# First two layers: pairs of column tiles with both parts of x in one matmul of 512 columns, and a quarter of the long convolution filtered on GpSimd

## The chip, the cores and the metric

The kernel runs on one core of one Trainium2 chip. The time is device microseconds of one launch, and lower is better. PE is TensorE, DVE VectorE, ACT ScalarE, POOL GpSimd, SP SyncE.

## The reference, cut to what matters

One sequence of 256 positions of width 2048 passes through four layers in fp32. The change touches the first two, which are alike:

```
h = rms_norm(x, norm_w[l])
p = h @ w_in[l]                                   # 2048 x 6668 columns
qa, ka, va, za, ub, zb, qkv_c, b_c, a_c, zc = _split_cols(p)
oa = sliding_window_sink_attention(...) * silu(za)
ob = conformer_conv_module(ub, ...) * silu(zb)    # depthwise convolution, 31 taps, 512 channels
oc = rms_norm(gated_deltanet(qkv_c, b_c, a_c, ...)) * silu(zc)
x = x + concatenate([oa, ob, oc]) @ w_out[l]

def conformer_conv_module(u, conv_w, conv_b, ln_w, ln_b, pw_w, pw_b):
    a, gt = jnp.split(u, 2, axis=-1)
    h = a * jax.nn.sigmoid(gt)
    h = causal_depthwise_conv(h, conv_w) + conv_b.astype(h.dtype)
    h = jax.nn.silu(layer_norm(h, ln_w, ln_b))
    return h @ pw_w + pw_b
```

Layers three and four (a pooling mixer and a gated linear recurrence, with their own large projections) are not touched.

## The kernel before, in words

**Precision by parts.** Every large product is fp32 made from two rounded parts of each factor. A weight chunk W (1 MB: four tiles of 128 rows by 512 columns, or eight by 256) comes by DMA from SP, ACT copies its upper part to WH (`high`, L1125), and DVE subtracts to get its lower part WL (`low`, L1818, over the same memory as W). The activations stand likewise as H: for each 128 rows kt, 256 columns of upper part (HH) and 256 of lower part (HL), side by side. A product is WL by HH plus WH by HL plus WH by HH.

**Two ways to issue it.** In mode "cm" of the class `Group` the weights are stationary and each of the three products is a matmul of 256 columns that adds to one half of a PSUM bank. So one tile of 128 by 128 weights takes three weight loads and three matmuls. Mode "wide" is used by the third and fourth layer: WL meets HH in a matmul of 256 columns, and WH meets both parts in one matmul of 512 columns, so a tile takes two loads and two matmuls, and two partial sums come out, which are added outside TensorE. A wide chunk runs all its WL matmuls and all its WH matmuls in two runs, with the order turned round from chunk to chunk.

**What runs in what order.** `plan()` lists 408 chunks, and every engine walks the list by itself. PE goes through a chunk and calls `pump()` four times in it; each call lets the side work (delta rule `delta_net`, `attention`, `conformer`, `decays`) issue its next small step, at a place counted with `rest(n)`. DVE and ACT have a `tick()` per chunk: first `low` or `high` for the chunk three ahead, then four pumps of their own side work. `group(n)` is n ticks and then a wait for the end of the chunk. All engines issue strictly in their own order, and wait on semaphores.

**PSUM.** The large products use bank pairs in turn by group number g. Group g + 2 may start when what was evicted from group g is done (`released`). In the first two layers a group of 512 columns is four chunks. DVE evicts it with `scaled` (L1783): one op of 128 by 512 for each bank, which multiplies by the row factors RBT of the normalisation. The side work has the other four banks.

**The convolution.** `conformer` on ACT starts the accumulator ACC, four tiles of 128 channels by 256 positions, with the last of the 31 taps, and DVE adds the other 30 taps with one `scalar_tensor_tensor` for each tile (L1787, out QA, in Q, TB, QA), one for each pump, at half that pace for the first 28. The layer's attention comes after it.

```
                for k in range(30):
                    for m in range(4):
                        wk = TB[:, wo + 4 * k + m:wo + 4 * k + m + 1]
                        stt(ACC[:, m, :], HB[:, m, k:k + 256], wk, ACC[:, m, :], ALU.mult, ALU.add, lag=3 if k else m)
                        yield
                        if 4 * k + m < 28:
                            yield
```

In the names of the profile Q and QA are large shared buffers: Q holds the values and masks of the side work, the pool and recurrence buffers, HB and RAW; QA holds ACC and the attention's q and k. SM holds small tiles.

Of the kernel before, what the change touches and what calls it, by code (L numbers as in the profile page):

```python
# [24 lines left out]
        "lo", "ev_v", "norm_v", "dn_v", "cf_v", "at_v", "y_v", "x_v", "uc_v", "d_v", "z_v", "step_v", "post_v")  # L25
# [7 lines left out]
def plan():  # L33
# [6 lines left out]

    for i in range(NP):
        ch.append(("w_in", 0, piece(i)[0], PIECES[i], 2048, 512))
    for l in range(2):
        for c in (2048, 2560)[1 - l:]:
            cols("w_in", l, c, 512)
        cols("w_vba", l, 0, 268)
        for c in (3584, 4096, 4608, 5120):
            cols("w_in", l, c, 512)
        cols("w_in", l, 5632, 256, step=8)
        cols("w_in", l, 5900, 512)  # L50
        cols("w_in", l, 6412, 256, step=8)
        for c in (3072, 0, 512):
            cols("w_in", l, c, 512)
        cols("w_in", l, 1280, 512)
# [193 lines left out]
def program(nc, wall, tab, pos_d, pT_d, xin, xT_d, gpost_d, gplo_d, xsave, out):  # L248
# [6 lines left out]
    with ctx:  # L255
# [10 lines left out]
        UL1 = ctx.enter_context(nc.sbuf_tensor("UL1", [128, 2, 256], F32R))  # L266
        QA = ctx.enter_context(nc.sbuf_tensor("QA", [128, 3584], F32))
# [45 lines left out]
        POOL_G, LRU_G = range(41, 84), range(93, 128)  # L313
        LAST_G = range(LRU_G.stop, LRU_G.stop + 8)

        def bank(g, b):
# [6 lines left out]
            return PS[:, 1024 * (g % 2) + 512 * b:1024 * (g % 2) + 512 * b + 512]  # L323

# [11 lines left out]
        DIAG = pair(SM[:, 704:960])  # L336
        ROPE = SM[:, 64:96]
# [112 lines left out]
        def tensor(e, w):  # L450
# [152 lines left out]

            def turn(n, i, *ready):
# [15 lines left out]
            def first_opening():  # L620
# [5 lines left out]
                def total():  # L626
                    yield from rest(1)
# [7 lines left out]
                g = Group(from_h, lambda kt: [hl_of(0, kt)], 512, "cm", 16)  # L635
                begin(total())
                g.feed(hi_first=True)
                g.all()
# [307 lines left out]
            def block1(l):  # L946
                if l:
                    opening(1, (3, "ev_v", 19))
# [17 lines left out]
                proj(l, 512)  # L966
# [4 lines left out]
                proj(l, 512)  # L971
                finish(cf)
                Group(lambda kt: ACC[:, kt, :], lambda kt: [("cf_a", l, "silu")], 512, "cm", 4).all()
                proj(l, 256)
# [10 lines left out]
                n, g16 = l + 1, 20 * l + 16  # L985
# [25 lines left out]
            def pool_layer():  # L1011
                assert here["g"] + 1 == POOL_G[0]

                def load_u(g):
                    if g:
                        proj(2, 512, "wide")
                    else:
                        opening(2, (3, "ev_v", 39))
# [82 lines left out]
        def scalar(e, w):  # L1101
# [61 lines left out]

            def skip(n):
# [22 lines left out]
            def entry(n):  # L1187
# [5 lines left out]
                g16 = 20 * n - 4  # L1193
# [155 lines left out]
            def attention(l):  # L1349
# [44 lines left out]
                w.wait_ge(*to("ev_v", 20 * l + 15))  # L1394
# [10 lines left out]
            def block1(l):  # L1405
                if l:
                    tick()
                    upper(1, 3)
                    sumsq(1, 3, SQX, X, ("ev_v", 19))
# [25 lines left out]
                cf = begin(conformer(l, skip(4)))  # L1435
# [11 lines left out]
                for i in range(5):  # L1447
                    g = skip(4 if i < 4 else 2)
# [4 lines left out]
                for k, (n, t0, t1) in enumerate(((4, 10, 14), (2, 14, 16))):  # L1453
                    begin(gate(Y[:, t0:t1, :], skip(n), "dn_a", l, "zc", k))
                begin(gate(Y[:, 6:10, :], skip(4), "cf_a", l, "zb"))
# [8 lines left out]
                skip(4)  # L1464
# [5 lines left out]
                group(2)  # L1470
# [5 lines left out]
                for k in (6, 8):  # L1476
                    ysplit(k, k // 2 - 3, "ev_v", 20 * l + 14)
# [45 lines left out]
            def pool_layer():  # L1523
# [240 lines left out]
        def vector(e, w):  # L1764
# [175 lines left out]

            def summed(dst, g):
# [174 lines left out]
            def conformer(l):  # L2116
# [15 lines left out]
                half = CFT[:, 0:512]  # L2132
                tt(half.rearrange("p (m c) -> p m c", m=2), ACC[:, 0:2, :], ACC[:, 2:4, :], ALU.add)
# [110 lines left out]
            def block1(l):  # L2244
# [5 lines left out]
                g = group(4)  # L2250
# [395 lines left out]
```

## Time and profile before

| what | value |
|---|---|
| median of 3 runs | 2366.91 us (2366.69 to 2366.96) |
| the profiled execution | 2367.18 us, of which the span is 2365.4 us |
| PE | 2346.3 us busy, 99% of the span |
| PE weight loads | 2091.4 us, 88% |
| DVE | 1675.6 us, 71% |
| ACT | 1283.1 us, 54% |
| POOL | 0.2 us |

The granted TensorE clock is 1.00 in every stretch read below. A busy share is the union of an engine's instructions; two engines that are busy at once are both counted.

### The profile page before, as it was taken

The numbers are of one execution on the slowest core, as the hardware profiler recorded it, in microseconds if no ns is written. First come the engines' busy times: TensorE is split into PE (matmuls) and PEld (weight loads), VectorE is DVE, ScalarE is ACT, GpSimd is POOL, SyncE is SP. The second block draws the span as 40 slices with busy tenths as digits, with TensorE's granted clock in tenths as the row PEclk, the third lists the DMA queues.
The fourth block names the chain that finished last, engine by engine and source line by source line (L and its number), as shares of the span: only waits on it lengthen the run. The fifth ranks groups of instructions, "written<-read, shape, count | busy, mean of one in ns | idle before, by whom it ended". The sixth has DMA issues, their size and how long they took to land.

```text
span 2365.4 us, 35787 instructions
## 1 busy us (share of the span) xinstructions
PE 2346.3 (99%) x15332; PEld 2091.4 (88%) x15332; DVE 1675.6 (71%) x1922; ACT 1283.1 (54%) x1434; POOL 0.2 (0%) x4
## 2 busy tenths in 40 slices
PE   9999999999999999999999999999999999999997
PEld 9999898899998988988888888888888888888886
DVE  7888768558986685667567576676668668678774
ACT  6554366545543655444434334475566575667573
POOL 0000000000000000000000000000000000000000
PEclk9999999999999999999999999999999999999999
DMA  7543334555533345555555555565455555555553
GB/s 266 204 179 132 120 143 156 191 217 186 179 125 124 136 170 196 187 192 193 187 190 196 189 185 195 193 221 194 145 196 183 191 196 186 188 196 187 202 204 119
DMA packets 64558, 428.03 MB, mean 181 GB/s; under 512 B 7184, under 2 KB 7824, under 8 KB 15504
## 3 DMA queue, kind: packets, MB, share of 16 engines
q1 hardware_dynamic: 61568, 414.48, 48.7%
q10 hardware_dynamic: 2832, 11.27, 1.3%
q8 instruction: 120, 1.97, 0.3%
q14 instruction: 38, 0.31, 0.0%
HBM read 421.53 MB, written 4.19 MB: 180 GB/s over the span
## 4 chain that ended last, share of the span: by engine, by line
PE 97%; DVE 2%; ACT 1%; issue 0%; DMA 0%; DVEq 0%; ACTq 0%
PE PS L456 95%; PE PS L616 1%; ACT Q L1111 1%; DVE Q L1783 0%; PE PS L914 0%; PE PS L748 0%; DVE X L1787 0%; PE PS L735 0%; DVE Q L1787 0%; PE PS L895 0%; DVE SM L1802 0%; DVE H L1783 0%; DVE E L1783 0%; DMA W<-in_wall 0%; ACT L1111 0%
## 5 line engine op out<-in xcount | busy, mean ns | idle before, releaser
L1818 DVE TENSOR_TENSOR WL<-W,WH 128x2048 fp32r<-128x2048 f32 (+3 forms) x406 | 887.7, 2194 | 453.9 <-ACT WH L1125 453.2
L1125 ACT ACTIVATE WH<-W 128x2048 fp32r<-128x2048 f32 (+3 forms) x406 | 740.9, 1836 | 492.1 <-PE PS L456 430.7
L456 PE MATMUL PS<-H,WH 128*128 128x256 f32 (+1 forms) x4864 | 868.9, 325 | 0.7 <-ACT H L1111 0.7
L456 PEld LDWEIGHTS PS<-H,WH 128*128 128x128 f32 x4864 | 740.7, 191 | 72.5 <-ACT WH L1125 0.8
L456 PE MATMUL PS<-H,WL 128*128 128x256 f32 x3392 | 491.3, 284 | 0.1
L456 PEld LDWEIGHTS PS<-H,WL 128*128 128x128 f32 x3392 | 446.5, 192 | 8.0 <-issue 1.8
L456 PE MATMUL PS<-WH,H 128*128 128x512 f32 (+1 forms) x1280 | 331.2, 379 | 0.0
L456 PEld LDWEIGHTS PS<-WH,H 128*128 128x128 f32 x1280 | 234.1, 188 | 46.0
L456 PE MATMUL PS<-WH,YS 128*128 128x512 f32 x1024 | 273.8, 389 | 0.0
L456 PEld LDWEIGHTS PS<-WH,YS 128*128 128x128 f32 x1024 | 192.2, 188 | 40.0
L456 PE MATMUL PS<-WL,H 128*128 128x512 f32 (+1 forms) x640 | 197.6, 388 | 0.1
L1111 ACT ACTIVATE Q<-PS 128x512 f32<-128x512 f32 (+3 forms) x134 | 68.9, 552 | 187.5 <-PE PS L456 119.4
L456 PE MATMUL PS<-WL,YS 128*128 128x512 f32 x512 | 157.8, 389 | 0.0
L456 PEld LDWEIGHTS PS<-WL,H 128*128 128x128 f32 x640 | 114.7, 188 | 22.6 <-issue 2.0
L456 PEld LDWEIGHTS PS<-WL,YS 128*128 128x128 f32 x512 | 95.5, 188 | 19.5 <-issue 0.2
L1787 DVE SCALAR_TENSOR_TENSOR QA<-Q,TB,QA 128x256 f32<-128x256 f32 x240 | 107.5, 477 | 0.1
L1783 DVE TENSOR_TENSOR Q<-Q,PS 128x512 f32<-128x512 f32 (+1 forms) x90 | 54.8, 648 | 63.3 <-ACT Q L1111 34.1
L1787 DVE SCALAR_TENSOR_TENSOR Q<-Q,TB 128x256 f32<-128x256 f32 x206 | 93.9, 491 | 7.7 <-ACT Q L1111 6.9
L456 PEld LDWEIGHTS PS<-Q 64*64 64x64 f32 (+2 forms) x1440 | 65.8, 149 | 9.7 <-issue 7.8
L1111 ACT ACTIVATE Q<-Q 128x1024 f32<-128x1024 f32 (+4 forms) x50 | 56.9, 1137 | 29.2 <-DVE Q L1792 11.8
L456 PE MATMUL PS<-Q 64*64 64x64 f32 (+2 forms) x1440 | 72.2, 240 | 0.0
L1111 ACT ACT_TABLE_LOAD x48 | 61.6, 1283 | 1.6
(164 smaller groups left out, 1634.9 us busy)
## 6 DMA issues: line engine op xcount, KB each, us to landing
W<-in_wall SPq DMA_DIRECT2D x374, 1024.0 KB, 4.8
W<-in_wall SPq DMA_DIRECT2D x22, 512.0 KB, 3.5
W<-in_wall SPq DMA_DIRECT2D x8, 536.0 KB, 3.4
X<-in_x ACTq DMA_DIRECT2D x1, 2048.0 KB, 9.5
xsave<-X ACTq DMA_DIRECT2D x1, 2048.0 KB, 8.5
X<-xsave ACTq DMA_DIRECT2D x1, 2048.0 KB, 9.7
Q<-in_g_post ACTq DMA_DIRECT2D x8, 256.0 KB, 3.5
Q<-in_g_ple_out ACTq DMA_DIRECT2D x2, 1024.0 KB, 4.5
```

The costliest lines, as they stand in the source:

```text
L456: return e.matmul(o, l, r, start=start, stop=stop, skip_group_check=True)
L616: o = e.transpose(b[:, 256 * j + 128 * t:256 * j + 128 * t + 128], X[:, t, c:c + 128], ident)
L1111: e.activation(o, a, f, **k).then_inc(*up(*sig))
L1125: e.activation(WH[:, s % NSPL, 0:m], W[:, c % NRAW, 0:m], ACT.Copy).then_inc(*up("hi", c))
L1783: e.tensor_tensor(o, a, b, op).then_inc(*after(sig))
L1787: e.scalar_tensor_tensor(out=o, in0=a, scalar=s, in1=b, op0=op0, op1=op1).then_inc(*after(sig))
L1818: e.tensor_tensor(WL[:, c % NRAW, 0:m], W[:, c % NRAW, 0:m], WH[:, s % NSPL, 0:m].bitcast(F32), ALU.subtract).then_inc(*up("lo", c))
```

## The change

In the first two layers every part of the input product (h by w_in) that was in mode "cm", but for the first 512 columns of each layer, becomes mode "wide" in groups of 256 columns: 19 such pairs of column tiles in each layer, 38 in all, of two chunks each. A chunk is then eight row tiles by 256 columns instead of four by 512; its bytes and the number of chunks stay. Groups for v, the decays, q, k and the output product stay as they were.

A pair is evicted by two engines. ACT copies the second half of both banks (the sum of WL by HH and WH by HL) to a new tile PART; DVE adds PART to the first half into the destination, and then multiplies the destination by RBT, two ops of 128 by 512 where there was one. PART has one buffer, so ACT's copy waits until DVE has used the last one. PE waits for the eviction of a group of 256 columns, two chunks long, where it was one of four chunks.

The fourth tile of the convolution is filtered by GpSimd: for each of 30 taps a `tensor_scalar` into a small tile TAP, and a `tensor_tensor` that adds it to the accumulator, each waiting for the one before. DVE keeps three tiles and its pace of pumps, and waits for GpSimd's last tap before it sums the tiles. One side step (`total`) is placed one pump later.

```diff
+    def pairs(l, c0):
+        for c in (c0, c0 + 256):
+            cols("w_in", l, c, 256, step=8)
...
+        PART = nc.alloc_sbuf_tensor_at("PART", [128, 2, 256], F32, offset=nc.sbuf_base - 4 * 512)
...
+        def both(g, k):
+            v = PS[:, 1024 * (g % 2):1024 * (g % 2) + 1024]
+            return v.rearrange("p (i k t) -> p i k t", i=2, k=2)[:, :, k, :]
...
+        TAP = SM[:, 704:960]
...
             # tensor
+            def pairs(n, ncols):
+                for _ in range(ncols // 256):
+                    proj(n, 256, "wide")
...
-                for _ in range(3):
-                    proj(l, 512)
+                pairs(l, 3 * 512)
                 finish(dc)
                 dn = begin(delta_net(l), first=True)
-                proj(l, 512)
-                proj(l, 256)
-                proj(l, 512)
-                proj(l, 256)
-                proj(l, 512)
+                pairs(l, 512 + 256 + 512 + 256 + 512)
                 proj(l, 512, "tm")
                 proj(l, 512, "tm")
...
             # scalar
+            def pairs(n):
+                for _ in range(n):
+                    g = group(2)
+                    if "pair" in here:
+                        w.wait_ge(*to("ev_v", here["pair"]))
+                    here["pair"] = g
+                    act(PART[:, :, :], both(g, 1), ACT.Copy, "ev_a", g)
+                return g
...
             # vector
+            def pairs(dst, n):
+                for b in range(n):
+                    g = group(2)
+                    w.wait_ge(*to("ev_a", g))
+                    tt(dst(b), both(g, 0), PART[:, :, :], ALU.add)
+                    tt(dst(b), dst(b), rb(2), ALU.mult, "ev_v", g)
...
                 for k in range(30):
                     for m in range(4):
-                        wk = TB[:, wo + 4 * k + m:wo + 4 * k + m + 1]
-                        stt(ACC[:, m, :], HB[:, m, k:k + 256], wk, ACC[:, m, :], ALU.mult, ALU.add, lag=3 if k else m)
+                        if m < 3:
+                            wk = TB[:, wo + 4 * k + m:wo + 4 * k + m + 1]
+                            stt(ACC[:, m, :], HB[:, m, k:k + 256], wk, ACC[:, m, :], ALU.mult, ALU.add,
+                                lag=2 if k else m)
                         yield
                         if 4 * k + m < 28:
                             yield
                 half = CFT[:, 0:512]
+                w.wait_ge(*to("tap_g", l, 29))
...
+        def gpsimd(e, w):
+            for l in range(2):
+                w.wait_ge(*to("near"))
+                w.wait_ge(*to("cf_v", l, "hb"))
+                w.wait_ge(*to("cf_a", l, "acc"))
+                for k in range(30):
+                    wk = AT["b_conv_w"] + 124 * l + 4 * k + 3
+                    if k:
+                        w.wait_ge(*to("tap_g", l, k - 1))
+                    e.tensor_scalar(TAP, HB[:, 3, k:k + 256], TB[:, wk:wk + 1], None, ALU.mult).then_inc(
+                        *up("mul_g", l, k))
+                    w.wait_ge(*to("mul_g", l, k))
+                    e.tensor_tensor(ACC[:, 3, :], ACC[:, 3, :], TAP, ALU.add).then_inc(*up("tap_g", l, k))
```

What moves is seen best in the engines' own orders. On PE, just ahead of the first layer's v and decay product, the "cm" rows of before read as follows (H is x, L456 the matmul helper, x the count of equal instructions):

```order
L456 MATMUL PS<-H,WL 128x256 x4
L456 MATMUL PS<-H,WH 128x256 x8
L456 MATMUL PS<-H,WL 128x256 x4
L456 MATMUL PS<-H,WH 128x256 x8
L646 MATMUL PS<-TB,RBT 128x128 x2
L456 MATMUL PS<-WL,H 128x268 x2
```

The same place now:

```order
L470 MATMUL PS<-H,WH 128x512 x24
L470 MATMUL PS<-H,WL 128x256 x32
L470 MATMUL PS<-H,WH 128x512 x32
L470 MATMUL PS<-H,WL 128x256 x16
L662 MATMUL PS<-TB,RBT 128x128 x2
L470 MATMUL PS<-WL,H 128x268 x2
```

Twelve matmuls for four tiles have become four of 256 and four of 512 columns, in long runs of one kind.

On DVE, in the delta rule of the first layer, the transposed keys (Q<-PS,SM) were followed at once by `low` and the solver's first step (Q<-PS,TB). Before:

```order
L1783 TENSOR_TENSOR Q<-PS,SM 128x512 x3
L1787 SCALAR_TENSOR_TENSOR QA<-Q,TB,QA 128x256 x2
L1783 TENSOR_TENSOR Q<-PS,SM 128x2x128 x6
L1787 SCALAR_TENSOR_TENSOR QA<-Q,TB,QA 128x256 x2
L1818 TENSOR_TENSOR WL<-W,WH 128x2048
L1783 TENSOR_TENSOR Q<-PS,TB 128x384 x2
```

Now:

```order
L1804 TENSOR_TENSOR Q<-PS,SM 128x512 x3
L1808 SCALAR_TENSOR_TENSOR QA<-Q,TB,QA 128x256 x2
L1804 TENSOR_TENSOR Q<-PS,SM 128x2x128 x6
L1808 SCALAR_TENSOR_TENSOR QA<-Q,TB,QA 128x256
L1804 TENSOR_TENSOR Y<-PS,PART 128x512
L1804 TENSOR_TENSOR Y<-Y,RBT 128x512
L1839 TENSOR_TENSOR WL<-W,WH 128x2048
L1804 TENSOR_TENSOR Q<-PS,TB 128x384 x2
```

One tap op is gone there, and a pair's eviction of two ops stands ahead of the solver's step. Twenty rows earlier another eviction has grown from one op to two.

On DVE in the first layer's attention, the third place, before (Y<-PS,RBT is the last eviction of the layer's input product, H<-Y,H the split of the mixer's output, Q<-PS,TB the next heads' scores):

```order
L1783 TENSOR_TENSOR Y<-PS,RBT 128x512
L1783 TENSOR_TENSOR H<-Y,H 128x2x256 x3
L1818 TENSOR_TENSOR WL<-W,WH 128x2048
L1787 SCALAR_TENSOR_TENSOR Q<-PS,TB 128x384 x4
```

Now:

```order
L1804 TENSOR_TENSOR Y<-PS,PART 128x512
L1804 TENSOR_TENSOR Y<-Y,RBT 128x512
L1804 TENSOR_TENSOR H<-Y,H 128x2x256 x3
L1839 TENSOR_TENSOR WL<-W,WH 128x2048
L1808 SCALAR_TENSOR_TENSOR Q<-PS,TB 128x384 x4
```

One op more stands ahead of the scores.

## Rows read from the trace of the kernel before

**Rows 1.** The page: span, busy time by engine, the chain that ended last

```profile
span 2365.4 us, 35787 instructions
PE 2346.3 (99%) x15332; PEld 2091.4 (88%) x15332; DVE 1675.6 (71%) x1922; ACT 1283.1 (54%) x1434; POOL 0.2 (0%) x4
PE 97%; DVE 2%; ACT 1%; issue 0%; DMA 0%; DVEq 0%; ACTq 0%
```

**Rows 2.** Waits of PE in the whole span: total us, times, longest

```profile
PE PS L616 <- DVE X L1787: 4.0, 1, 4.0
PE PS L456 <- DVE RBT L1810: 1.2, 1, 1.2
```

**Rows 3.** Timeline of PE in a "cm" group: start us, us, instructions, count

```profile
500.47 1.12 PE L456 MATMUL PS<-H,WH 128*128 128x256 f32 x8
...
501.91 0.76 PE L456 MATMUL PS<-H,WH 128*128 128x256 f32 x5
```

**Rows 4.** Timeline of PE in "wide" groups of the third layer

```profile
1106.79 4.00 PE L456 MATMUL PS<-H,WL 128*128 128x256 f32 x32
1110.62 7.44 PE L456 MATMUL PS<-H,WH 128*128 128x512 f32 x32
1117.91 2.31 PE L456 MATMUL PS<-H,WL 128*128 128x256 f32 x18
```

**Rows 5.** Groups by form: count, busy us, mean ns, idle before

```profile
L1787 DVE SCALAR_TENSOR_TENSOR QA<-Q,TB,QA 128x256 f32<-128x256 f32 x240 | 107.5, 477 | 0.1
...
L1111 ACT ACTIVATE Q<-PS 128x512 f32<-128x512 f32 x84 | 46.1, 597 | 116.4 <-PE PS L456 89.1 <-PE PS L914 18.1 <-PE PS L895 9.1
...
L1783 DVE TENSOR_TENSOR Y<-PS,RBT 128x512 f32<-128x512 f32 x20 | 13.1, 687 | 7.6 <-PE PS L456 6.6
...
L1792 DVE TENSOR_SCALAR Q<-Q,TB 128x256 f32<-128x256 f32 x32 | 9.1, 347 | 0.0
...
L1783 DVE TENSOR_TENSOR Q<-PS,SM 128x256 f32<-128x256 f32 x12 | 4.2, 416 | 0.2
```

**Rows 6.** Windows of layer one: length, PE, PEld, DVE, ACT, POOL, clock, DMA

```profile
60.00:120.00 60.00, 60.00 (x503) 60.00 (x502) 50.94 (x90) 32.10 (x39) 0.00 (x0) 1.00 0.53 195
120.00:160.00 40.00, 40.00 (x335) 40.00 (x335) 33.50 (x51) 16.82 (x13) 0.00 (x0) 1.00 0.50 185
160.00:200.00 40.00, 40.00 (x305) 37.13 (x304) 33.00 (x53) 28.06 (x25) 0.00 (x0) 1.00 0.44 158
200.00:245.00 45.00, 45.00 (x470) 44.47 (x471) 43.38 (x62) 14.46 (x11) 0.00 (x0) 1.00 0.35 124
```

**Rows 7.** Timeline: first op on the convolution's accumulator, and the sum of its tiles

```profile
60.07 2.08 ACT L1111 ACTIVATE QA<-Q,TB 128x256 f32<-128x256 f32 x4 [0.22 <-DVE Q L1783]
...
312.10 0.69 DVE L1783 TENSOR_TENSOR Q<-QA 128x512 f32<-128x512 f32 x1
```

**Rows 8.** Timeline, ACT and DVE splitting one weight chunk

```profile
108.55 1.92 ACT L1125 ACTIVATE WH<-W 128x2048 fp32r<-128x2048 f32 x1 [3.84 <-PE PS L456]
...
110.50 2.29 DVE L1818 TENSOR_TENSOR WL<-W,WH 128x2048 fp32r<-128x2048 f32 x1 [1.09 <-ACT WH L1125]
```

**Rows 9.** Timeline at the decays: last softplus op, first matmul on it

```profile
80.48 0.17 DVE L1783 TENSOR_TENSOR SM<-SM 128x12 f32<-128x12 f32 x1
...
83.58 0.51 PE L456 MATMUL PS<-SM,TB 128*128 128x12 f32 x4
```

**Rows 10.** Timeline at the solver's first step

```profile
242.27 1.01 DVE L1783 TENSOR_TENSOR Q<-PS,TB 128x384 f32<-128x384 f32 x2
...
244.24 0.97 PE L456 MATMUL PS<-Q 64*64 64x64 f32 x26
```

**Rows 11.** Timeline at attention's first transposes

```profile
350.92 0.76 DVE L1798 COPY Q<-QA 128x512 f32<-128x512 f32 x2
...
352.83 0.60 PE L895 MATMUL PS<-TB,QA 128*128 128x128 f32 x4
```

**Rows 12.** Timeline at attention's transposed weights, with the wait before

```profile
378.67 0.67 PEld L914 LDWEIGHTS PS<-TB,Q 128*128 128x128 f32 x6 [0.17 <-DVE Q L1787]
```

More of the change, by code:

```diff
@@ L43, in plan @@
     for l in range(2):
-        for c in (2048, 2560)[1 - l:]:
-            cols("w_in", l, c, 512)
+        if l:
+            cols("w_in", l, 2048, 512)
+        pairs(l, 2560)
         cols("w_vba", l, 0, 268)
         for c in (3584, 4096, 4608, 5120):
-            cols("w_in", l, c, 512)
[L49 to L54, printed above, removed]
+            pairs(l, c)
+        cols("w_in", l, 5632, 256, step=8)
+        pairs(l, 5900)
+        cols("w_in", l, 6412, 256, step=8)
+        pairs(l, 3072)
+        for c in (0, 512):
+            cols("w_in", l, c, 512)
+        pairs(l, 1280)
         cols("b_pw_w", l, 0, 512, nkt=4)
@@ L626, in total @@
                 def total():
-                    yield from rest(1)
+                    yield from rest(2)
                     b = side(("norm", 0, "rb"), ("norm_a", 0, "rb"))
@@ L951, in block1 @@
                 if l:
-                    proj(l, 512)
+                    pairs(l, 512)
                 else:
@@ L1434, in block1 @@
                 skip(1)
-                cf = begin(conformer(l, skip(4)))
+                cf = begin(conformer(l, pairs(2)))
                 if not l:
@@ L1463, in block1 @@
                 att = begin(attention(l))
-                skip(4)
+                pairs(2)
                 finish(cf)
@@ L1469, in block1 @@
                 skip(1)
-                group(2)
+                pairs(1)
                 def ysplit(k, lag, *ready):
@@ L2249, in block1 @@
                     rp = begin(rope_tables())
-                g = group(4)
+                pairs(lambda b: Y[:, 6 + 2 * b:8 + 2 * b, :], 2)
                 if not l:
                     finish(rp)
-                scaled(lambda b: Y[:, 6 + 2 * b:8 + 2 * b, :], g)
                 if not l:
@@ L2266, in block1 @@
                 for i in range(5):
-                    g = group(4 if i < 4 else 2)
-                    scaled(lambda b: RAW[:, 4 * i + 2 * b:4 * i + 2 * b + 2, 3:259], g, 2 if i < 4 else 1)
+                    pairs(lambda b: RAW[:, 4 * i + 2 * b:4 * i + 2 * b + 2, 3:259], 2 if i < 4 else 1)
                     begin(taps(l, i, 4 if i < 4 else 2))
@@ L2273, in block1 @@
                 for n, t0 in ((4, 10), (2, 14)):
-                    scaled(lambda b: Y[:, t0 + 2 * b:t0 + 2 * b + 2, :], group(n), n // 2)
-                scaled(lambda b: Y[:, 6 + 2 * b:8 + 2 * b, :], group(4))
+                    pairs(lambda b: Y[:, t0 + 2 * b:t0 + 2 * b + 2, :], n // 2)
+                pairs(lambda b: Y[:, 6 + 2 * b:8 + 2 * b, :], 2)
                 group(4)
@@ L2279, in block1 @@
                 att = begin(attention(l))
-                scaled(lambda b: Y[:, 2 * b:2 * b + 2, :], group(4))
+                pairs(lambda b: Y[:, 2 * b:2 * b + 2, :], 2)
                 finish(cf)
@@ L2291, in block1 @@
                         lag=m)
-                scaled(lambda b: Y[:, 4:6, :], group(2), 1)
+                pairs(lambda b: Y[:, 4:6, :], 1)
                 def add_x(i, g):
```

41 lines of the change are left out of this document (21 added, 20 removed).

## The prediction, made blind

> **What bounds the kernel now.** The page comes first. PE is busy for 2346.3 us of a span of 2365.4, and the chain that ended last lies on it for 97% [rows 1]. The reader should still ask whether this busy engine is a waiting one, since an engine's busy time can hide stalls that others cause. The list of PE's waits answers: beside the start and the end, the two longest kinds are 4.0 and 1.2 us, one wait each [rows 2]. So TensorE works without a break, and every other engine is late only where nobody sees it. What shortens PE's own stream shortens the kernel, as long as the others still keep out of its way. That second half is the hard one here. DVE is busy for 43.38 of the 45 us from 200 to 245 [rows 6], so there it has no room, and the places where PE takes over a DVE result have little to spare [rows 9 to 12]. These are read by eye from the timeline: when the DVE op ends, and when PE's matmul that needs it starts.
>
> **Part 1, fewer matmuls.** In a "cm" group twelve matmuls, four tiles' worth, come every 1.44 us, from 500.47 to 501.91 [rows 3]. That is 360 ns a tile. In a "wide" group 32 matmuls of 256 columns begin at 1106.79, 32 of 512 at 1110.62, and the next run at 1117.91 [rows 4]: 11.12 us for 32 tiles, 347.5 ns a tile. The reader can take the pieces apart: 120 ns for 256 columns, 228 for 512. The streamed columns are the same 768, so only the share that each matmul carries beyond its columns is saved, 12.5 ns a tile. The change moves 38 pairs of column tiles by 16 row tiles, which is 1216 tiles: 1216 x 12.5 ns = 15.2 us. A chunk of 16 tiles then takes 5.56 us instead of 5.76.
>
> The Trainium skill (TensorE: Matmul & The Clock Gate, Back-to-back issue gap) gives an isolated warm matmul N / 2.4 + about 2.5 ns, so a matmul saved would be worth 2.5 ns, and the 1216 would give 3.0 us instead of 15.2. The rows, with a weight load for every matmul, show 13 to 14 ns over the columns' own time at both sizes, so by them the larger figure stands.
>
> **Part 2, the evictions.** A bank cost DVE one op: 13.1 us for 20, 0.655 each [rows 5]. A pair costs two that depend on each other, of 687 ns each and a little for the handover, 1.4 us. Nineteen pairs for each layer add 19 x (1.4 - 0.655) = 14.2 us to DVE. ACT gains 19 copies of 597 ns [rows 5], 11.3 us, and has the room: 32.10 busy of 60 us, 16.82 of 40, 28.06 of 40, 14.46 of 45 [rows 6]. The release of PSUM is not in danger by size: a group lasts 11.1 us now, and copy and two ops need 2.0. It would be late only with DVE 9 us behind.
>
> **Part 3, the taps.** DVE loses 30 taps for each layer. 240 taps take 107.5 us, 0.448 each [rows 5], so 13.4 us. Evictions and taps nearly cancel over a layer, +0.8 us. They don't cancel everywhere: from 60 to 160 us DVE does only 28 of the 120 taps, so it loses 7 (3.1 us) while eight pairs come (6.0 us), and PE is 16 x 0.2 = 3.2 us faster through it. DVE's spare time there, 9.1 + 6.5 = 15.6 us [rows 6], becomes 9.5; from 160 to 200 it has 7.0, less 1.2 for the faster PE. That leaves 15 us for what GpSimd does to it.
>
> **Part 4, GpSimd.** It begins when ACT has started the accumulator, at about 62 us, and has until the tiles are summed at 312 [rows 7], 250 us for 30 taps or 8.3 us each; even at three times DVE's price it is done in time. The trace has no tensor op on POOL (0.2 us, four instructions [rows 1]), so what it does to DVE is bounded: below, nothing; above, every one of the 60 ops holds DVE back for as long as DVE would take for such an op, 347 ns and 416 ns [rows 5], 0.76 us a tap and 23 us a layer. I take 0.4 us a tap, 12 us a layer, the middle of the two bounds, since no row lies nearer to the one than to the other. It fits in the 15 us, barely.
>
> The weight parts forgive this. ACT starts on a chunk at 108.55 and DVE has finished at 112.79 [rows 8]; three chunks of 5.76 lie between, so PE needs it at 125.8, 13.0 us later. With chunks of 5.56, ACT's copy and the longer eviction, 10.4 remain.
>
> **Part 5, the places that don't forgive**, for each layer:
> - Decays: DVE ends at 80.65, PE starts at 83.58, 2.9 us to spare [rows 9]. PE comes 0.6 earlier (three chunks). The softplus ahead is some fifteen short DVE ops in a chain, just when GpSimd is at work; if 9 or 10 of them are held up for 0.38 us, half of the two ops of a tap together, they end 3.5 us later. PE waits 1.2.
> - Solver: DVE ends at 243.28, PE starts at 244.24, 0.96 to spare [rows 10]. Since 200 DVE had no room. It gains 0.1, 0.75 and 1.4 us of evictions and loses about six taps, 2.7 us; PE is 7 x 0.2 = 1.4 us earlier. About 0.3 with ACT's handover.
> - Attention's transposes: 351.68 to 352.83, 1.15 to spare [rows 11]. PE is 0.8 earlier, and ACT's copy of 0.6 stands in the chain that leads there. 0.25.
> - Attention's weights: PE waits 0.17 us already [rows 12]. One op more (0.75) and PE two chunks (0.4) earlier, less what the wait itself rounds off: 1.0.
>
> Sum: 2.75 us a layer, 5.5 for both. 15.2 - 5.5 = 9.7. The profiled execution took 2367.18 us, its span and 1.8 around it, so 2357.5; it stands 0.27 over the median of the runs, so **2357.2 us**.
>
> **The rivals.**
> *Full gain.* DVE takes none of it back, or the waits fall where PE would have waited anyway. 2366.9 - 15.2 = 2351.7. For it: half of the places have ACT or DVE idle just ahead. Against: the wait that is there already [rows 12].
> *GpSimd eats it.* Each tap delays DVE 0.65 us, 20 a layer, 5 more than it has. The delay stands at 200, where DVE can't work it off, and the solver's steps wait for it: about 4.5 us a layer beyond mine, 2366.
> *GpSimd turns it round.* The same mechanism, past its point. From 15 us on, each us of delay in a layer is a us of PE; the gain is gone at 15 + 9.7 / 2 = 20 us a layer, 0.66 us a tap, and the kernel is measurably slower from about 22. If a GpSimd op takes half as long again as DVE's, and always collides, a tap costs 1.14 us, a layer 34, which is 19 over: 2357.2 + 38 = 2395. With the upper bound above it is 2373. For it: the window 60 to 120 is 85% busy with ops that read two SBUF tensors. Against: GpSimd slows itself down in the same way, so that its ops spread out.
> The Trainium skill (SBUF — State Buffer, Who interferes with whom) says that DVE instructions with two SBUF inputs contend with GpSimd instructions that read SBUF, and that the loser blocks for the whole instruction. No row of this trace shows it. The Trainium skill (GPSIMD Engine Reference, 3.1 Elementwise — side-by-side cycle accounting) has the GpSimd's `tensor_tensor` at 1.96 times DVE's time; by both together this rival would be the likeliest, which is why it has the chance it has.
> *The matmuls save little.* 3 us less the waits, 2369. The spacing of the matmuls speaks against it [rows 3, 4], and nothing here for it.
>
> **How the numbers follow.** My forecast 0.62, its own range 2352 to 2362; full gain 0.10; GpSimd eats it 0.14; turns it round 0.11; little saved 0.03. A measurement of this kernel can tell 0.2%, 4.7 us, from no change, so 2362.2 to 2371.6 is the same. Faster: 0.62 + 0.10 = 0.72. Same: 0.14 + 0.03 = 0.17. Slower: 0.11. The range runs from 2351 (the full gain) to 2370, which leaves out the case turned round and the edge of the one before it.
>
> **What would show it.** Right: PE rows of 512 columns 228 ns apart in layers one and two, PE's busy time 8 to 15 us less, new waits of PE on DVE of about a us at the four places. Wrong: waits of PE on WL at 100 to 200 us, or waits in the solver of several us, with DVE's mean for its taps well above 477 ns while POOL is busy. If the pitch of the 512 column matmuls in these layers were 240 ns, part 1 would be wrong.

## The result, and the profile after

The changed kernel takes 2382.92 us (median of four runs, 2382.53 to 2384.25), and the kernel before 2366.89. The ratio is 1.0069, with a 95% interval of 1.0058 to 1.0081. It is 16 us slower where 9.7 us faster was forecast.

The page's totals answer to [rows 1]:

```profile
span 2380.7 us, 33530 instructions
PE 2340.5 (98%) x14116; PEld 2029.4 (85%) x14116; DVE 1706.3 (72%) x1900; ACT 1299.8 (55%) x1472; POOL 153.3 (6%) x124
PE 79%; DVE 13%; ACT 4%; issue 3%; DMA 1%; DVEq 0%; ACTq 0%
```

PE was idle for 19.1 us of the span before and is for 40.2 now, 21.1 more. Its busy time fell by only 5.8. The difference of the two is what the span grew by, 15.3. The chain that ended last lay on PE for 97% and now does for 79%; DVE's part rose from 2% to 13%. The waits of PE, in us in total, times and longest, answer to [rows 2]:

```profile
PE PS L470 <- DVE Q L1804: 9.3, 12, 2.0
PE PS L470 <- ACT Q L1122: 6.7, 2, 3.3
...
PE PS L930 <- DVE Q L1808: 2.3, 4, 0.8
PE PS L751 <- DVE Q L1804: 2.0, 2, 1.0
...
PE PS L470 <- DVE SM L1804: 1.1, 1, 1.1
```

The matmuls did what they should. In the first layer a wide chunk runs as in [rows 4], 7.28 us from the first of 32 matmuls of 512 columns to the next run:

```profile
93.56 7.44 PE L470 MATMUL PS<-H,WH 128*128 128x512 f32 x32
100.84 3.34 PE L470 MATMUL PS<-H,WL 128*128 128x256 f32 x26
```

GpSimd's ops by form:

```profile
L2619 POOL TENSOR_SCALAR SM<-Q,TB 128x256 f32<-128x256 f32 x60 | 92.2, 1537 | 459.8 <-ACT QA L1122 454.1
L2622 POOL TENSOR_TENSOR QA<-QA,SM 128x256 f32<-128x256 f32 x60 | 60.9, 1015 | 5.0
```

It was at work in the first layer from 63.2 to 145.1 us. Here is the window of 62 to 144 us (the columns are those of [rows 6]), and then the same window of the kernel before:

```profile
62.00:144.00 82.00, 78.45 (x460) 69.59 (x459) 72.10 (x99) 41.77 (x47) 75.54 (x59) 0.98 0.51 185
```

```profile
62.00:144.00 82.00, 82.00 (x687) 82.00 (x686) 68.02 (x117) 42.13 (x46) 0.00 (x0) 1.00 0.51 186
```

GpSimd did its 30 taps of the layer back to back, in 82 us. What this cost DVE is read from its groups by form in that window (count, busy us, mean ns), which answer to the means of [rows 5]:

```profile
L1839 DVE TENSOR_TENSOR WL<-W,WH 128x2048 fp32r<-128x2048 f32 x14 | 35.3, 2523 | 6.7 <-ACT WH L1136 6.7
L1808 DVE SCALAR_TENSOR_TENSOR QA<-Q,TB,QA 128x256 f32<-128x256 f32 x20 | 12.2, 627 | 0.0
L1808 DVE SCALAR_TENSOR_TENSOR Q<-Q,TB 128x256 f32<-128x256 f32 x17 | 11.1, 685 | 0.0
L1804 DVE TENSOR_TENSOR Q<-Q,RBT 128x512 f32<-128x512 f32 x5 | 3.9, 789 | 0.2
L1804 DVE TENSOR_TENSOR Q<-PS,PART 128x512 f32<-128x512 f32 x5 | 3.5, 692 | 1.5 <-ACT PART L1122 1.0
...
L1808 DVE SCALAR_TENSOR_TENSOR SM<-SM 128x12 f32<-128x12 f32 x9 | 2.8, 310 | 0.3
```

In the kernel before, the same window has 2288, 477, 477 and 171 ns for the first, second, third and last of these forms. 14 x 0.235, 20 x 0.150, 17 x 0.208, 5 x 0.1 and 9 x 0.139 us make 11.6. Summed over every op of DVE, each against the median of its form without GpSimd, it is 13.4 us in the layer, 0.45 a tap. The expectations below say 13.7. The op that reads a PSUM bank and one SBUF tile, `Q<-PS,PART`, takes 692 ns with GpSimd busy or not.

Where the time went is seen best in PE's progress. PE raises a semaphore at the end of each chunk; its times in the trace, as us behind (+) or ahead (-) of the kernel before at the same chunk, are these. The first layer ends in chunk 79. Each row is of the profiled execution. That of "pairs only" took 2369.50 us, 2.6 under the median of its runs, so its row shows less loss than the median has.

```
chunk                 17     29     33     37     45     66    104    112    120    150
before, ends at     65.1  137.3  160.3  188.5  252.1  410.4  604.4  655.6  719.3  917.4
the changed kernel   0.0   +2.9   +3.1   +6.8   +7.8   +8.0   +7.4  +14.4  +15.3  +15.5
pairs only          -0.3   -2.7   -3.5   -1.6   +2.0   +2.3   -0.9   -1.0   +2.6   +2.9
GpSimd only          0.3    0.7    0.7    0.7    0.7    0.7    1.1    1.1    1.1    1.1
no fourth tile      +0.7   -1.7   -2.5   -3.3   -2.5   -2.2   -5.4   -7.0   -6.2   -5.9
fourth tile late    +0.3   -2.1   -3.0   -3.7   -2.6   -2.4   -5.6   -7.2   -6.1   -5.8
ACT order            0.1   +3.0   +2.2   +2.3   +3.3   +3.5   +4.4   +3.7   +4.7   +5.0
gap in the solver   +0.5   -1.9   -2.7   -3.5   -4.2   -4.5   -7.7   -9.3  -10.0  -10.3
```

Where nothing is in the way, each four chunks bring 0.8 us, 0.2 a chunk, as the prediction had it. The changed kernel loses its time in steps, at the chunks 21, 28, 37 and 42 to 45, and again in the second layer.

### The profile page after: what moved, and what is told of

The parts are those of the page before. It is cut to its first block, busy times and chain, and to the rows that moved or that the text cites. A ratio compares the mean times of both kernels' runs of the same rounds, so it can differ in the third digit from the quotient of the medians.

```text
span 2380.7 us, 33530 instructions
## 1 busy us (share of the span) xinstructions
PE 2340.5 (98%) x14116; PEld 2029.4 (85%) x14116; DVE 1706.3 (72%) x1900; ACT 1299.8 (55%) x1472; POOL 153.3 (6%) x124
## 4 chain that ended last, share of the span: by engine, by line
PE 79%; DVE 13%; ACT 4%; issue 3%; DMA 1%; DVEq 0%; ACTq 0%
PE PS L470 77%; DVE WL L1839 3%; DVE Q L1804 3%; DVE Q L1808 2%; ACT Q L1122 2%; DVE QA L1808 2%; ACT WH L1136 1%; PE PS L634 1%; DMA W<-in_wall 1%; DVE Y L1804 1%; DVE SM L1823 0%; ACT QA L1122 0%; DVE QA L1804 0%; DVE Q L1815 0%; DVE SM L1808 0%
## 5 line engine op out<-in xcount | busy, mean ns | idle before, releaser
L470 PE MATMUL PS<-H,WH 128*128 128x512 f32 (+1 forms) x3648 | 807.0, 376 | 0.3 <-ACT H L1122 0.3
L470 PEld LDWEIGHTS PS<-H,WH 128*128 128x128 f32 x3648 | 649.6, 189 | 118.1 <-issue 0.7
L470 PE MATMUL PS<-H,WL 128*128 128x256 f32 x3392 | 444.6, 284 | 8.1 <-DVE Q L1804 7.5
L470 PEld LDWEIGHTS PS<-H,WL 128*128 128x128 f32 x3392 | 428.5, 192 | 20.0 <-issue 10.3
L470 PE MATMUL PS<-WH,H 128*128 128x512 f32 (+1 forms) x1280 | 331.2, 379 | 0.0
L470 PE MATMUL PS<-WH,YS 128*128 128x512 f32 x1024 | 273.8, 389 | 0.0
L470 PEld LDWEIGHTS PS<-WH,H 128*128 128x128 f32 x1280 | 234.1, 188 | 45.9
L470 PEld LDWEIGHTS PS<-WH,YS 128*128 128x128 f32 x1024 | 192.2, 188 | 40.0
L470 PE MATMUL PS<-WL,H 128*128 128x512 f32 (+1 forms) x640 | 197.7, 388 | 0.0
L1122 ACT ACTIVATE Q<-PS 128x512 f32<-128x512 f32 (+3 forms) x134 | 68.9, 552 | 182.1 <-PE PS L470 118.2
L470 PE MATMUL PS<-WL,YS 128*128 128x512 f32 x512 | 157.8, 389 | 0.0
L470 PEld LDWEIGHTS PS<-WL,H 128*128 128x128 f32 x640 | 114.7, 188 | 22.7 <-issue 2.0
L2619 POOL TENSOR_SCALAR SM<-Q,TB 128x256 f32<-128x256 f32 x60 | 92.2, 1537 | 459.8 <-ACT QA L1122 454.1
L470 PEld LDWEIGHTS PS<-WL,YS 128*128 128x128 f32 x512 | 95.5, 188 | 19.5 <-issue 0.2
L1808 DVE SCALAR_TENSOR_TENSOR Q<-Q,TB 128x256 f32<-128x256 f32 x206 | 100.3, 531 | 7.7 <-ACT Q L1122 6.9
L1804 DVE TENSOR_TENSOR Q<-Q,PS 128x512 f32<-128x512 f32 (+1 forms) x90 | 54.9, 649 | 61.6 <-ACT Q L1122 34.1
L1808 DVE SCALAR_TENSOR_TENSOR QA<-Q,TB,QA 128x256 f32<-128x256 f32 x180 | 88.3, 512 | 0.1
L470 PEld LDWEIGHTS PS<-Q 64*64 64x64 f32 (+2 forms) x1440 | 65.9, 149 | 12.8 <-issue 10.5
L470 PE MATMUL PS<-Q 64*64 64x64 f32 (+2 forms) x1440 | 72.4, 240 | 1.7 <-DVE Q L1804 1.7
L1122 ACT ACTIVATE Q<-Q 128x1024 f32<-128x1024 f32 (+4 forms) x50 | 56.9, 1137 | 30.2 <-DVE Q L1813 11.8
```

The lines of the kernel that those rows point to most:

```text
L470: return e.matmul(o, l, r, start=start, stop=stop, skip_group_check=True)
L1122: e.activation(o, a, f, **k).then_inc(*up(*sig))
L1804: e.tensor_tensor(o, a, b, op).then_inc(*after(sig))
L1808: e.scalar_tensor_tensor(out=o, in0=a, scalar=s, in1=b, op0=op0, op1=op1).then_inc(*after(sig))
L2619: e.tensor_scalar(TAP, HB[:, 3, k:k + 256], TB[:, wk:wk + 1], None, ALU.mult).then_inc(*up("mul_g", l, k))
```

## The experiments

Theory A was that GpSimd's burst alone did it, theory B that the eviction by two engines did. Theories C and D came from the first four runs. Each time stands beside that of the kernel before on the same chip.

**Pairs only.** GpSimd's function is left out and DVE filters all four tiles:

```diff
-                        if m < 3:
-                            ... lag=2 if k else m)
+                        stt(ACC[:, m, :], HB[:, m, k:k + 256], wk, ACC[:, m, :], ALU.mult, ALU.add, lag=3 if k else m)
-                w.wait_ge(*to("tap_g", l, 29))
```

> The changed kernel without its GpSimd part: DVE filters all four tiles again, the 38 pairs stay. Theory A (the burst): GpSimd does its 30 taps of a layer back to back in 82 us, its collisions cost DVE 13.7 us there, DVE falls behind and everything that waits for it is late. Without GpSimd the pairs then bring nearly what their matmuls save, 15.5 us, less waits of some us where DVE is full (200 to 245 us): 2354 to 2358 us. Theory B (the eviction by two engines): two DVE ops and a copy through one PART buffer, with PE waiting two chunks later, is itself what stalls PE, and GpSimd adds little: 2372 or more, with PE's waits on released banks at 127 to 175 us still there.

Measured: 2372.12 us beside 2366.95, ratio 1.0019 (1.0010 to 1.0028). Neither theory's number. The waits on released banks are gone, so B as stated falls; but the pairs alone lose 5 us, and A had them win about 10.

**GpSimd only.** The groups of before, with GpSimd's function, the loop of three tiles and the wait for its last tap from the change.

> The kernel before, with only the fourth convolution tile moved to GpSimd; groups stay as they were. Theory A: the same 60 GpSimd ops a layer collide just as much, DVE is lengthened by 12 to 14 us between 60 and 145 us of the layer, less the 3 us of its taps that went; the 13 us of spare time there just take it, so PE waits little: 2366 to 2370 us. Theory B: GpSimd's share of the loss is small anyhow: 2365 to 2367 us. The split of DVE's lengthening (is it 13.7 us without the pairs too?) is the reading that matters here.

Measured: 2366.86 beside 2366.95, ratio 1.0000 (0.9991 to 1.0008). That lies in both theories' ranges, so the time alone does not tell them apart. The collisions are all there:

```profile
L1820 DVE TENSOR_TENSOR WL<-W,WH 128x2048 fp32r<-128x2048 f32 x15 | 37.0, 2469 | 7.0 <-ACT WH L1127 7.0
L1789 DVE SCALAR_TENSOR_TENSOR Q<-Q,TB 128x256 f32<-128x256 f32 x22 | 14.6, 696 | 0.0
L1789 DVE SCALAR_TENSOR_TENSOR QA<-Q,TB,QA 128x256 f32<-128x256 f32 x21 | 13.8, 673 | 0.0
```

They are 14.9 us in the layer, op by op, and PE does not feel them. So 5 and 0 become 16 only together. That each half takes the room that the other needs is the likely reading; the later runs bear it out.

**No fourth tile.** As the changed kernel, GpSimd's function and the wait for it left out. The fourth tile keeps its first tap only, so a part of the convolution isn't computed.

> The changed kernel with GpSimd's part left out and the fourth tile of the convolution left with its first tap only (its output is therefore not the reference's). DVE has the relief and no collision. Theory A: about 2352 us, the full saving of the matmuls. Theory B: 2370 or more, since the eviction is as in the changed kernel.

Measured: 2360.00 beside 2366.95, ratio 0.9970 (0.9958 to 0.9981). A's sign, not its size: with DVE relieved and nobody colliding, 8 of 15 us are still missing. Its waits of PE say where:

```profile
PE PS L930 <- DVE Q L1808: 2.3, 4, 0.8
PE PS L751 <- DVE Q L1804: 2.0, 2, 1.0
PE PS L470 <- DVE Q L1804: 1.6, 2, 0.8
```

They stand in the solver and ahead of the attention's weights.

**Paced.** GpSimd waits before tap k:

```diff
                 for k in range(30):
+                    w.wait_ge(*to("chunk", (17, 92)[l] + k))
```

> The changed kernel with GpSimd paced: tap k waits for the end of the chunk 17 + k (92 + k in the second layer), so the 30 taps are spread over some 200 us in place of 82. Theory A: the total of DVE's lengthening stays 10 to 14 us a layer, but the spare time of 60 to 200 us takes most of it: 2358 to 2366 us. Theory B: no change, 2380 to 2384 us. If only the sum of collisions counted and not their density, it would also stay near 2383.

Measured: 2380.15, ratio 1.0054 (1.0041 to 1.0068). A falls: the taps are spread over 200 us, and almost nothing comes back. It is the number of B, but B alone had fallen with the first run. Its largest wait of PE has moved to the start of the delta rule:

```profile
186.76 3.78 PE L470 MATMUL PS<-Q,TB 128*128 128x512 f32 x4 [4.04 <-ACT Q L1122]
```

Two theories come from these four. C: what counts is when DVE is loaded. D: DVE and ACT hold each other up in a ring. The next rows are why. In the changed kernel, first ACT, then DVE, from 150 us, when GpSimd has long finished:

```profile
151.98 1.71 ACT L1122 ACTIVATE Q<-Q,TB 128x256 f32<-128x256 f32 x4 [9.05 <-DVE Q L1804]
153.78 1.06 ACT L1122 ACTIVATE Q<-Q 128x1024 f32<-128x1024 f32 x1
154.75 1.90 ACT L1136 ACTIVATE WH<-W 128x2048 fp32r<-128x2048 f32 x1
```

```profile
150.53 0.69 DVE L1804 TENSOR_TENSOR Q<-PS,PART 128x512 f32<-128x512 f32 x1
151.25 0.69 DVE L1804 TENSOR_TENSOR Q<-Q,RBT 128x512 f32<-128x512 f32 x1
151.86 2.29 DVE L1839 TENSOR_TENSOR WL<-W,WH 128x2048 fp32r<-128x2048 f32 x1
154.06 1.27 DVE L1808 SCALAR_TENSOR_TENSOR QA<-Q,TB,QA 128x256 f32<-128x256 f32 x3
156.68 2.29 DVE L1839 TENSOR_TENSOR WL<-W,WH 128x2048 fp32r<-128x2048 f32 x1 [1.35 <-ACT WH L1136]
```

The reader follows it in a circle. ACT stands for 9.05 us in `taps`, waiting for DVE's late eviction. Behind it in ACT's order is `high`, the copy to WH. ACT has been idle since 142.9. The copy could have started at 146.40, when PE ended chunk 30, and yet it starts only at 154.75; now DVE, which is late, has to wait 1.35 us for it. So DVE idles while it is behind, and does not catch up. In the kernel before the same ACT op waits 0.4 to 1.2 us.

**ACT order.** The changed kernel, with that op of ACT one chunk later for four of five groups, behind the next `high`:

```diff
             def taps(l, i, n, g):
-                yield
+                yield from rest(5 if i < 4 else 1)
...
-                yield from rest(3 * n + 6)
+                yield from rest(3 * n + 2 if i < 4 else 3 * n + 6)
```

> The changed kernel with one edit in ACT's order: the first operation of the delta rule's short filters, which waits for DVE's eviction, stands one chunk later, behind the next weight part's copy. In the changed kernel ACT stood idle for 9 us at it with that copy queued behind, and DVE then waited 1.35 us for the copy. Theory D (DVE and ACT hold each other up in a ring): DVE catches up after GpSimd's taps, and the time falls by 3 to 8 us, to 2375 to 2380. Theory C alone (DVE's load): 2382 to 2384, unchanged, and if ACT becomes late with the filters, more.

Measured: 2371.89 beside 2366.79, ratio 1.0021 (1.0012 to 1.0029), 11 us less than the changed kernel. D is shown, and is worth more than expected. GpSimd still works in a burst (to 147.7 us) and collides as much (14.1 us), but the window of 120 to 160 us has DVE busy for 39.23 us, where the changed kernel had 35.73; first the changed kernel, then this run:

```profile
120.00:160.00 40.00, 37.40 (x201) 32.49 (x200) 35.73 (x42) 20.28 (x21) 23.50 (x19) 0.96 0.47 163
```

```profile
120.00:160.00 40.00, 37.98 (x207) 33.26 (x206) 39.23 (x48) 19.97 (x20) 26.08 (x19) 0.96 0.48 174
```

Of DVE's 4.3 idle us 3.7 were waits for `high`; in this run none are. PE's waits of 3.3 us for ACT at the delta rule's start are 0.6 to 0.7 us now, and all its waits in the row `PE PS L470 <- DVE Q L1804` fall from 9.3 to 5.9 us.

**Same pace.** The changed kernel, GpSimd's tap k held back to about DVE's tap k:

```diff
+                    w.wait_ge(*to("chunk", (17, 92)[l] + (2 * k if k < 5 else k + 5)))
```

> The changed kernel with GpSimd's tap k held back until about where DVE does its own tap k (a tap for every two chunks at first, then one a chunk, last one after chunk 51 of the layer). Theory C: the lengthening of DVE stays at 13 to 15 us a layer and now stands where the relief of 13.4 us stands, so both cancel and the time is that of the run with pairs and no GpSimd, 2369 to 2375 us. If a collision costs more than it lasts, because it meets ops that others wait for (the solver's), 2378 us or more.

Measured: 2380.06, ratio 1.0051 (1.0037 to 1.0065), the higher of the two numbers, and a miss for C. DVE was lengthened by less than expected here, 9.5 us in the first layer and 11.0 in the second, so it is not the sum of collisions that keeps the time up. **Pace and ACT order** is the same with the edit to `taps`:

> GpSimd at DVE's pace, with the same edit in ACT's order. Theory C and D together: with the ring open, collisions and relief cancel, and the time is that of the run with pairs, no GpSimd and the same order, within 3 us. Its own stall at 182 us (4.0 us for ACT) goes: 2361 to 2368. If collisions cost more than they last, because of what they hit: 2372 or more.

Measured: 2366.41 beside 2367.20, ratio 0.9998 (0.9989 to 1.0007), in the expected range. **Pairs and ACT order** has DVE filter all tiles, with the edit:

> Pairs with all four tiles on DVE at their old places and no GpSimd, plus the edit in ACT's order of the run before (the short filters' first operation one chunk later). Theory D: the loss of the pairs alone was the ring too (ACT idled 7 us at 159 to 166, PE then waited 2.4 us for it at 183 and the clock fell at 216), so it turns from 5 us over the kernel before into a gain: 2361 to 2366 us. If DVE's plain load was the cause, 2370 to 2373, unchanged.

Measured: 2367.79 beside 2367.20, ratio 1.0002 (0.9993 to 1.0011), above the 2361 to 2366 expected, but 4 us below the pairs alone. Here are the differences of these medians to the kernel before, in us; each is uncertain by 2 to 3 us:

```
                          ACT's order as it was    with the edit
pairs, all on DVE                 +5.2                  +0.6
GpSimd at DVE's pace             +13.3                  -0.8
GpSimd at once (the change)      +16.0                  +5.1
```

Read down the second column: with the ring open, that is with the edit that breaks it, GpSimd's collisions cost about what the taps relieve (-0.8 beside +0.6), and the burst costs some 6 us more. That this is because it comes before the relief is argued from its place. Read across: the ring is worth 5, 14 and 11 us, more where GpSimd makes DVE late. What is left of the pairs' loss stands at DVE in the solver. Of the pairs with ACT's order, these are PE's two waits there in the first layer, and then the window:

```profile
213.07 2.02 PE L470 MATMUL PS<-Q 128*128 128x128 f32 x16 [1.99 <-DVE Q L1804]
235.46 1.77 PE L751 MATMUL PS<-TB,Q 128*128 128x128 f32 x8 [2.19 <-DVE Q L1804]
```

```profile
200.00:245.00 45.00, 40.83 (x323) 36.27 (x323) 44.01 (x64) 13.65 (x13) 0.00 (x0) 0.96 0.28 98
```

**Fourth tile late.** Pairs, no GpSimd, ACT's order as it was. DVE does the fourth tile's taps behind the others', from the 22nd on:

```diff
+                        j = 4 * (k - 21) + m
+                        if 0 <= j < 30:
+                            stt(ACC[:, 3, :], HB[:, 3, j:j + 256], wk, ACC[:, 3, :], ALU.mult, ALU.add,
+                                lag=1 if m < 3 else 0)
```

> Pairs as in the changed kernel, GpSimd unused; DVE filters three tiles at their old places, and the 30 taps of the fourth tile stand behind them in DVE's order from the 22nd tap on (about 252 to 312 us of the layer). Theory C (what counts is when DVE is loaded: until 245 us it has no room, in 245 to 320 it idles 27 of 75 us): the 13.4 us of taps are hidden there, and the time is that of the run that left the tile out, 2358 to 2362 us. If DVE's total load counted, or the solver's steps had no room for 0.4 us ahead of them, it would be the 2372 us of the run with all four tiles on DVE.

Measured: 2361.72 beside 2366.79, ratio 0.9977 (0.9968 to 0.9987). C holds. The 13.4 us of taps a layer cost 1.7 us in all over the run that left them out (2360.00), by the medians, which is within the uncertainty of the two. The window of 245 to 320 us takes them; before, then this run:

```profile
245.00:320.00 75.00, 75.00 (x879) 63.70 (x876) 47.52 (x70) 30.90 (x36) 0.00 (x0) 1.00 0.33 124
```

```profile
245.00:320.00 75.00, 75.00 (x839) 62.17 (x838) 55.42 (x87) 32.79 (x40) 0.00 (x0) 1.00 0.32 113
```

**Last 256 columns as before.** The same, and columns 1792 to 2047 in mode "cm" with one DVE op (`proj(l, 256)` on PE, `group(2)` on ACT, `scaled(..., group(2), 1)` on DVE).

> As the run with the fourth tile late on DVE, and the last group of 256 columns of each layer's input product (columns 1792 to 2047) is again issued with separate 256-column matmuls and evicted by one DVE op. It gives up 0.4 us of TensorE a layer and takes one op of 0.7 us and a wait for ACT out of DVE's order ahead of the attention's scores. Theory C: PE's waits on DVE there (1.1 us a layer) fall to 0.3, so the time is 0.5 to 1.5 us below that run. If these waits have another cause it is 0.8 us above.

Measured: 2360.28, ratio 0.9971 (0.9959 to 0.9982). 1.4 us less, as expected, though no more than the two runs' spread. The wait for the attention's weights is the shown part: 2.2 us in four waits became 0.7 in two.

**Solver's groups as before.** In addition the three groups of columns 5900 to 6667:

> As the run with the fourth tile late and the last 256 columns of the product by separate matmuls, and three more groups of 256 columns for each layer (5900 to 6667, those that DVE evicts ahead of and in the solver) issued so too. It gives up 3 x 0.4 = 1.2 us of TensorE a layer and takes three DVE ops of 0.7 us from the stretch of 189 to 245 us, where DVE is full and PE waits 0.8 and 1.0 us. Theory C: the waits go, 2.3 us a layer with what restarting costs, so 1 us a layer is left: 2357 to 2360. If the waits move to the next step of the solver, 2361 to 2363.

Measured: 2359.43 beside 2367.20, ratio 0.9967 (0.9955 to 0.9980). The wait of 0.8 us went, that of 1.0 became 0.5, and the 2.4 us given up on PE ate what that brought. No difference to the run before that can be told.

**Gap in the solver.** Fourth tile late and the last 256 columns as before; no taps on DVE from the 15th to the 21st, and all that are left in the 36 steps from the 22nd on:

```diff
+                        if k < 14:
+                            if m < 3:
+                                tap(m, k, 2 if k else m)
+                        elif i >= 0:
+                            for t in later[13 * i // 6:13 * (i + 1) // 6]:
+                                tap(*t, 1)
```

> As the run with the fourth tile late and the last 256 columns by separate matmuls, but DVE does no taps at all from the 15th to the 21st (about 190 to 250 us of the layer, the solver's first half), and does the 27 + 21 + 30 taps that are left in the 36 steps from the 22nd on (about 252 to 312 us). Theory C: DVE has 9 us more room where PE waits for it (0.8, 1.0 and 0.2 us), so these waits go, and 31 us of taps with 39 of other work fit in the 76 us that follow: 2355 to 2358 us. If the steps of the solver that stand between the taps come late there, new waits at 250 to 310 us of the layer: 2361 us or more.

Measured: 2356.97 beside 2366.81, ratio 0.9958 (0.9944 to 0.9971). This is the fastest version, 9.8 us ahead of the kernel before. DVE's room has moved to where PE waits for it, and of the solver's three waits in a layer one is left:

```profile
200.00:245.00 45.00, 44.49 (x390) 39.17 (x388) 38.94 (x53) 13.11 (x12) 0.00 (x0) 1.00 0.34 119
245.00:320.00 75.00, 75.00 (x838) 62.07 (x838) 61.01 (x104) 34.33 (x41) 0.00 (x0) 1.00 0.32 113
```

```profile
231.25 1.25 PE L751 MATMUL PS<-TB,Q 128*128 128x128 f32 x8 [0.51 <-DVE Q L1804]
```

## Why the prediction was wrong

**Part 1 was right.** 228 ns for 512 columns, 0.2 us a chunk. The figure of the Trainium skill (TensorE: Matmul & The Clock Gate, Back-to-back issue gap) for an isolated matmul, about 2.5 ns beyond its columns, would have given 0.04 us a chunk. It does not fit this stream.

**Part 4's price was right, and its sum wrong.** 0.4 us a tap, 12 a layer, was forecast; 13.4 was measured. There is luck in that. The upper bound charged each GpSimd op with DVE's time for it, 0.35 and 0.42 us, and the shortest that GpSimd took were 0.92 and 0.72, so the bound was none, and its middle no more than a good guess. The step that failed is "it fits in the 15 us, barely". It failed twice. First, these 15 us were counted up to 200 us, but GpSimd, which after the accumulator's start waits for nobody, had finished by 145. Up to 144 DVE had had 14 us of idle time (82 less 68.02), of which the prediction's own working had already given some 6 to the pairs and the faster PE. Second, that idle time was not spare. The busy share says how long an engine did nothing, not that it could have worked: DVE was waiting for ACT's `high` then, and once DVE was late ACT waited for DVE in turn. The run with ACT's order shows the part of the ring: 11 of the 16 us.

Forecast and result lie 25.7 us apart. One way from the result back to the forecast goes through the runs: opening the ring takes off 11 us (+16.0 to +5.1), holding GpSimd to DVE's pace 6 (to -0.8), and doing the taps on DVE, but out of the solver's stretch, with the last 256 columns as before, 9 (to -9.8). Another order of the steps would share it out otherwise.

A count in part 3 was off as well. From 60 to 160 us the kernel before has 43 of the 120 tap operations, not 28. That made DVE's room look some 1.7 us smaller than it was, so it doesn't explain the loss.

**Part 2 had the danger and dismissed it.** "It would be late only with DVE 9 us behind." It was. The eviction of chunks 24 and 25, which ended at 114.10, began on DVE at 125.55, 11.4 us later, and PE, which needed the banks for chunk 28, waited for it:

```profile
125.55 0.69 DVE L1804 TENSOR_TENSOR Q<-PS,PART 128x512 f32<-128x512 f32 x1
```

```profile
127.27 2.80 PE L470 MATMUL PS<-H,WL 128*128 128x256 f32 x16 [2.02 <-DVE Q L1804]
```

The next one, of chunks 26 and 27, began 13.6 us after their end (125.27, 138.86), and PE waited again, for 0.15 to 0.4 us each, at every second chunk until 175. The prediction's signs of being wrong had waits for WL in this stretch and not for banks; of these signs only the mean of the taps (627 ns) came true.

**Part 5's list was short by its worst place.** It named hand-overs from DVE to PE only. At the delta rule's start PE waits for ACT to read its sums (L1122, `Q<-PS,TB`), and ACT came there late because its order runs through DVE's eviction. ACT first, then PE:

```profile
186.57 0.91 ACT L1122 ACTIVATE Q<-Q,TB 128x256 f32<-128x256 f32 x2 [1.72 <-DVE Q L1804]
187.39 1.89 ACT L1136 ACTIVATE WH<-W 128x2048 fp32r<-128x2048 f32 x1
189.30 1.28 ACT L1126 ACT_TABLE_LOAD   x1
190.59 3.01 ACT L1122 ACTIVATE Q<-PS,TB 128x512 f32<-128x512 f32 x5
```

```profile
191.34 1.99 PE L470 MATMUL PS<-Q,TB 128*128 128x512 f32 x4 [3.34 <-ACT Q L1122]
```

Of the four places that it did name, the decays waited 1.1 us (1.2 forecast) in the first layer, the solver 0.9 and 1.0 (0.3), the transposes 0.2 (0.25), the weights 1.1 (1.0). In the run without a fourth tile, which has no collision, the solver's waits are the same 0.8 and 1.0. So GpSimd does not make them. The evictions' second op does, in part: with the solver's groups evicted by one op the 0.8 went and the 1.0 became 0.5.

**A wait costs more than it lasts.** The prediction charged waits at face value. PE's idle time rose by 21.1 us, and its busy time fell by 5.8 in place of 15.5 (38 pairs, two chunks each, 0.204 us a chunk), so 9.7 us more went. A chunk with a wait of 0.15 to 0.42 us took 0.22 to 0.24 us beyond the wait and its 5.57 us (the chunks 30, 32, 34 and 36). The longer waits at the chunks 21 and 37 cost 0.26 each beyond themselves, against the run without a fourth tile. PE has 22 more waits than before, so some 5 us, by estimate. And twice the granted clock fell from 2.4 to 1.2 GHz for 3.4 us, just after a wait and at the end of one. Over 4 us it is 0.57 in the mean:

```profile
128.00:132.00 4.00, 4.00 (x18) 3.57 (x18) 2.82 (x3) 3.91 (x6) 3.72 (x4) 0.57 0.35 147
664.00:668.00 4.00, 3.48 (x5) 1.58 (x6) 3.90 (x6) 2.89 (x5) 0.00 (x0) 0.57 0.00 0
```

At 0.57 of the speed for 4 us each is worth up to 1.7 us. Of the 9.7 us some 1 to 2 are left without an account. The first fall came after 2.0 us of waiting at 125.3, the second at the end of the second layer's wait of 3.3 us at 661; in the first layer the wait of 3.3 us that ended at 191 left the clock at 1.00, so these runs don't tell what decides it.

**The rivals.** "GpSimd turns it round" had the sign, with a threshold of 20 us of collisions a layer. The measured 13.4 are far below it, and GpSimd alone cost nothing, so the mechanism was another: the pairs, the burst and ACT's order together. No case had that. The contention itself is there, as below, yet the price of a tap was not what decided.

## What to carry to other kernels

Idle time of an engine is room only if what it waits for does not wait for it. Before you spend it, look at the order of the engine that it waits for, and at what stands there behind an op that needs yours: in this kernel one op of ACT for each of four groups, one chunk later, was worth 11 us. Place extra work by the stretch, not by the total: the same 13 us of taps a layer cost 12 us in all at one place in DVE's order (2372.12 beside 2360.00) and 1.7 at another (2361.72), and an engine that waits for nobody does its work in a burst, earlier than you need it. For places without room look at the hand-overs of all engines to the one that bounds, and charge each wait of TensorE with its restart.

## What the runs showed of the hardware

**Two engines, one at a time.** Three early ops of GpSimd in the changed kernel, and DVE's beside them:

```profile
65.22 2.85 POOL L2619 TENSOR_SCALAR SM<-Q,TB 128x256 f32<-128x256 f32 x1
68.14 0.74 POOL L2622 TENSOR_TENSOR QA<-QA,SM 128x256 f32<-128x256 f32 x1
68.98 2.84 POOL L2619 TENSOR_SCALAR SM<-Q,TB 128x256 f32<-128x256 f32 x1
```

```profile
64.82 2.45 DVE L1839 TENSOR_TENSOR WL<-W,WH 128x2048 fp32r<-128x2048 f32 x1 [1.32 <-ACT WH L1136]
...
68.20 2.83 DVE L1839 TENSOR_TENSOR WL<-W,WH 128x2048 fp32r<-128x2048 f32 x1
```

A GpSimd op of 0.93 us (the shortest of its form is 924 ns) that starts at 65.22 ends at 68.07: all but 0.13 us of it comes after DVE's subtraction is through, at 67.27. The next subtraction takes 2.83 us in place of 2.29, since the GpSimd op at 68.14 was first: it ends 2.15 us after that one, again its own time less 0.14. In the whole burst every `tensor_scalar` that met a subtraction that had begun before it ended 0.79 to 0.80 us after it, eight times.

This agrees with the Trainium skill (SBUF — State Buffer, Who interferes with whom): a DVE instruction with two SBUF inputs contends with a GpSimd instruction that reads SBUF, and the shared port pair is an exclusive lock. It also says that a DVE instruction with at most one SBUF input, outside its 2-port modes, does not contend; here the op that reads PSUM and one SBUF tile keeps its 692 ns.

Free of collisions GpSimd's `tensor_tensor` took 0.74 us, where DVE takes 0.416 for the shape with one input in PSUM, 1.8 times as long, and its `tensor_scalar` 0.93 beside 0.347, 2.7 times [rows 5]. The Trainium skill (GPSIMD Engine Reference, 3.1 Elementwise — side-by-side cycle accounting) has 1.96 for `tensor_tensor` with 2048 elements a partition, which this trace with 256 nearly bears out.

**Relief and collision cancel.** A tap of 256 elements took 0.448 us off DVE and gave 0.45 us back in collisions in the burst, and 0.37 at DVE's own pace with the ring open. Most of DVE's work in these stretches reads two SBUF tiles. Moving the tap to GpSimd brought nothing that can be told from no change even at its best (2366.41 beside 2367.79).
